# Two chained transformer models in one kernel: root tables loaded a stage ahead, norm sums before a low half, and three smaller moves

## The reference, cut to what matters

```
first_block:  h = x + short_conv_mixer(rms_norm(x));   h += conv_ffn(rms_norm(h))          # layer 0
              shared = shared_latent_kv(h)                                                # k, v, rotated key part
              h += mla_attention(rms_norm(h), shared);  h += conv_ffn(rms_norm(h))         # layer 1
              x = rms_norm(h) * final
second_block: mod = silu(c) @ w_ada + b_ada            # 6 vectors: shift, scale, gate, twice
              h = rmsnorm(x) * (1 + scale1) + shift1;  proj = h @ w_in
              y = [gated mix a | stick-breaking b | dilated windows c] @ w_out
              x += (1 + gate1) * y;  then a conv feed-forward with shift2, scale2, gate2
              out = rmsnorm(x) * g_final
rms_norm(x, g) = x * rsqrt(mean(x*x) + 1e-6) * g
```

## Time and profile before

| | |
|---|---|
| median of three runs | 1773.13 us |
| profiled execution | 1772.59 us |
| its span, first to last instruction | 1770.8 us |
| instructions | 21953 |
| TensorE busy | 97% |
| VectorE, ScalarE, GpSimd busy | 64%, 39%, 22% |
| mean granted clock of TensorE | 0.988 |
| HBM traffic | 105 GB/s |
| weight tiles | 291 x 512 KB, 3.3 us from issue to landing |

### The profile page before, as it was taken

The page is one execution under the profiler, slowest core; times in us unless marked ns, Lnnn a source line. Parts: engine busy times, 40 slices in busy tenths (PEclk is TensorE's granted clock), DMA queues, the critical chain, the costliest instruction groups (busy, mean ns, idle before and its releaser), DMA issues.

```text
span 1770.8 us, 21953 instructions
## 1 busy us (share of the span) xinstructions
PE 1719.7 (97%) x7798; PEld 1392.7 (79%) x7798; DVE 1131.6 (64%) x1438; ACT 682.6 (39%) x919; POOL 395.4 (22%) x170
## 2 busy tenths in 40 slices
PE   7999999999999999999999999999989899999997
PEld 6888788888887776878888888788647788888886
DVE  5566777776666786577777666564755677777222
ACT  4123444443324335344444322432553444444221
POOL 3444100000444430310000144444202200000443
PEclk9999999999999999999999999899999899999999
DMA  5233233223664220132332366322101232233331
GB/s 185 95 107 99 94 100 98 95 95 130 217 211 143 85 83 1 60 107 95 98 101 98 122 241 213 115 91 88 60 1 48 68 98 95 95 96 101 99 108 71
DMA packets 52042, 186.25 MB, mean 105 GB/s; under 512 B 5776, under 2 KB 5904, under 8 KB 51984
## 3 DMA queue, kind: packets, MB, share of 16 engines
q1 hardware_dynamic: 50832, 182.47, 31.0%
q10 hardware_dynamic: 1152, 2.99, 0.5%
HBM read 183.35 MB, written 2.10 MB: 105 GB/s over the span
## 4 chain that ended last, share of the span: by engine, by line
PE 89%; DVE 7%; ACT 2%; issue 1%; DMA 1%; DVEq 0%; ACTq 0%; POOL 0%; SPq 0%
PE ps L1505 27%; PE ps L1506 27%; PE ps L1507 27%; PE ps L1718 1%; PE ps L1744 1%; PE ps L1640 1%; PE ps L1642 1%; PE ps L1641 1%; DVE RAB L1080 1%; PE ps L1725 1%; DMA X<-x_in 1%; DVE acc L892 1%; PE ps L1733 0%; DVE QXL L903 0%; DVE cstat L1426 0%
## 5 line engine op out<-in xcount | busy, mean ns | idle before, releaser
L495 POOL TENSOR_TENSOR WL<-raw,WH 128x1024 fp32r<-128x1024 f32 x157 | 384.3, 2448 | 1327.7 <-ACT WH L544 1327.7
L1505 PE MATMUL ps<-XH,WH 128*128 128x512 f32 x1496 | 587.5, 393 | 15.6 <-DVE XL L903 10.2
L1506 PE MATMUL ps<-XL,WH 128*128 128x512 f32 x1496 | 583.6, 390 | 0.0
L1507 PE MATMUL ps<-XH,WL 128*128 128x512 f32 x1496 | 583.5, 390 | 0.0
L544 ACT ACTIVATE WH<-raw 128x1024 fp32r<-128x1024 f32 x291 | 308.7, 1061 | 586.5 <-PE ps L1507 551.2
L1505 PEld LDWEIGHTS ps<-XH,WH 128*128 128x128 f32 x1496 | 281.9, 188 | 79.4 <-POOL WL L495 9.8
L1507 PEld LDWEIGHTS ps<-XH,WL 128*128 128x128 f32 x1496 | 281.8, 188 | 58.9
L1506 PEld LDWEIGHTS ps<-XL,WH 128*128 128x128 f32 x1496 | 282.0, 188 | 58.6 <-issue 1.0
L1507 PE MATMUL ps<-HH,WL 128*128 128x512 f32 x528 | 205.4, 389 | 0.0
L1506 PE MATMUL ps<-HL,WH 128*128 128x512 f32 x528 | 205.4, 389 | 0.0
L1505 PE MATMUL ps<-HH,WH 128*128 128x512 f32 x528 | 205.4, 389 | 0.0
(11 more groups left out here) (262 smaller groups left out, 1905.7 us busy)
## 6 DMA issues: line engine op xcount, KB each, us to landing
raw<-w_tiles SPq DMA_DIRECT2D x291, 512.0 KB, 3.3
ada<-ada_tiles SPq DMA_DIRECT2D x32, 512.0 KB, 5.4
trig<-ada_tiles SPq DMA_DIRECT2D x16, 512.0 KB, 7.1
out_x<-X SPq DMA_DIRECT2D x8, 256.0 KB, 2.0
X<-x_in ACTq DMA_DIRECT2D x2, 512.0 KB, 8.2
X<-x_in SPq DMA_DIRECT2D x2, 512.0 KB, 8.5
RAB<-c_in SPq DMA_DIRECT2D x2, 512.0 KB, 4.6
MK<-mask_in ACTq DMA_DIRECT2D x1, 576.0 KB, 4.6
```

The costliest lines, as they stand in the source:

```text
L495: nc.gpsimd.tensor_tensor(WL[k % SPL][:, :], raw[:, k, :], f32(WH[k % SPL][:, :]), ALU.subtract).then_inc(s_lo, 1)
L1505: mm(bank, h, xh, start=first, stop=False)
L1506: mm(bank, h, xl, start=False, stop=False)
L1507: return mm(bank, lo, xh, start=False, stop=last)
```

## The change

Nothing is computed differently; instructions are moved.

1. Root's table is loaded explicitly before `residual` of DN0, WO, DN1, OUT2 and DN2, where before it came with the root itself.
2. At the end of DN1 and OUT2 the low half of the next stage's second tile comes after the reciprocal of the norm. The modulation vectors come before the last eviction of DN1 (`last=vectors`). Three DMA issues on ScalarE come after the root.
3. The masks are made after the first reciprocal of the kernel. TensorE starts attention once the first two `QN` are evicted and waits for the others from the third block on.
4. The eviction t = 3, j = 0 of UKV comes ahead of the last two `XL`.
5. In IN2 the second angle moves from k = 5 to k = 7. On ScalarE `Sin` moves from k = 6 to 8 and `Gelu` from 7 to 5.

```diff
@@ ScalarE
             up(0, "UP0", False)
+            nc.scalar.preload_act_table(ACT.Sqrt)
             residual("DN0", 3, "kv_in", N_KV)
...
             up(1, "UP1", False)
+            nc.scalar.preload_act_table(ACT.Sqrt)
             residual("DN1", 3, None, N_FIN, second=True)
+
+            act.wait_ge(s_ms, 1)
+            nc.scalar.activation(nt[:, 2:4, :], nt[:, 0:2, :], ACT.Sqrt, scale=1.0 / D).then_inc(s_root, 1)
 
             act.dma_start(MK[:, :], mask_in.bitcast(BF16)).then_inc(s_in["mask"], 16)
             act.dma_start(WS[:, :, :], wsp_in).then_inc(s_in["wsp"], 16)
             act.dma_start(posi[:, :], pos_in).then_inc(s_in["pos"], 16)
-
-            act.wait_ge(s_ms, 1)
-            nc.scalar.activation(nt[:, 2:4, :], nt[:, 0:2, :], ACT.Sqrt, scale=1.0 / D).then_inc(s_root, 1)
...
-                if k == 6:
+                if k == 8:
...                 (the two Sin)
-                if k == 7:
+                if k == 5:
...                 (the two Gelu)
@@ VectorE
+                        if last is not None and m == KD - 1:
+                            last()
                         product(M, i, per)
...
                             early_sums(n)
-                            if then is not None:
-                                low(then, 0)
                             continue
...
             inverse(N_A, rb)
+            dve.wait_ge(s_in["const"], 16)
+            v.tensor_copy(mask16[:, 0, :], cc("ident")).then_inc(s_m16, 1)
+            v.tensor_copy(mask16[:, 1, :], cc("causal_neg")).then_inc(s_m16, 1)
+            v.tensor_copy(mask16[:, 2, :], cc("strict_neg")).then_inc(s_m16, 1)
...
             for t in range(HEADS // 2):
                 for j in range(4):
+                    if (t, j) != (3, 0):
+                        latent_out(t, j)
...
                     for m in range(KQ):
+                        if m == KQ - 2:
+                            latent_out(3, 0)
                         lo_half(XH[:, m, :], XL[:, m, :], QL[:, m, :], vcol("q_norm", m), (s_lh, KKV + m + 1), s_ll)
...
-            residual("DN1", 3, None, None, N_FIN, modulation=1, second=True, then=T0["IN2"] + 1)
+            residual("DN1", 3, None, None, N_FIN, modulation=1, second=True, last=vectors)
...
             v.reciprocal(nt[:, 4:6, :], nt[:, 2:4, :]).then_inc(s_dg, 1)
+            low(T0["IN2"] + 1, 0)
             dve.wait_ge(s_bc, 2)
...
-                if k == 5:
+                if k == 7:
                     angle(RB, 0.25)
                     ch.link(v.memset(acc[:, :], 0.0))
...
-            residual("OUT2", 1, None, None, N_F2, gate=2, then=T0["UP2"] + 1)
+            residual("OUT2", 1, None, None, N_F2, gate=2)
 
             whole_sums(N_F2)
             token_inverse(N_F2)
+            low(T0["UP2"] + 1, 0)
@@ TensorE
-            pe.wait_ge(s_ev, M0["WO"])
+            pe.wait_ge(s_ev, M0["UQ"] + HEADS // 2 + 2)
             pe.wait_ge(s_m16, 3)
             for a in range(BLOCKS_A + 4):
+                if a == 2:
+                    pe.wait_ge(s_ev, M0["WO"])
```

More of the change, by code:

```diff
@@ L929, in whole_sums, with residual @@
                 v.tensor_tensor(nt[:, 0, :], nt[:, 6, :], ps[4][:, 0:4], ALU.add).then_inc(s_ms, 1)
-            def residual(phase, tiles_per_m, e, gname, n, gate=None, modulation=None, second=False, then=None):
+            def residual(phase, tiles_per_m, e, gname, n, gate=None, modulation=None, second=False, last=None):
                 per = 4 * tiles_per_m
@@ L1151, in key_rope, with latent_out @@
                     ropes[0] += 1
+            def latent_out(t, j):
+                M = M0["UKV"] + 4 * t + j
+                product(M)
+                if t < 2:
+                    v.tensor_copy(KN[:, 4 * t + j, :], ps[M % 4][:, :]).then_inc(s_ev, 1)
+                else:
+                    g = V_GROUP * (t - 2)
+                    v.tensor_copy(VT[:, g:g + V_GROUP, j * P:(j + 1) * P],
+                                  ps[M % 4][:, :].rearrange("p (h d) -> p h d", h=V_GROUP)).then_inc(s_ev, 1)
             for t in range(HEADS // 2):
                 for j in range(4):
[L1155 to L1162, removed]
+                    if (t, j) != (3, 0):
+                        latent_out(t, j)
                 if t == 0:
@@ L1181, in _ @@
                     key_rope(h - 1)
[L1184 to L1187, removed]
             def half_lo(n):
@@ L1238, in _, with vectors @@
             dve.wait_ge(s_cact, 2)
-            residual("DN1", 3, None, None, N_FIN, modulation=1, second=True, then=T0["IN2"] + 1)
[L1241 to L1247, removed]
-                ch.link(v.tensor_scalar(gm[:, row, :], mod[:, part * KD:(part + 1) * KD], 1.0, None, ALU.add))
-            ch.link(v.tensor_tensor(gm[:, 0, :], gm[:, 0, :], vec[:, V["final"][0]:V["final"][0] + KD], ALU.mult))
+            def vectors():
+                dve.wait_ge(s_ada, 6 * KD)
+                b0 = V["b_ada"][0]
+                ch.link(v.tensor_tensor(mod[:, :], mod[:, :], vec[:, b0:b0 + 6 * KD], ALU.add))
+                for row, (part, g) in enumerate(((1, "g_mix"), (4, "g_ffn"))):
+                    ch.step(v.scalar_tensor_tensor(gm[:, row, :], mod[:, part * KD:(part + 1) * KD], 1.0,
+                                                   vec[:, V[g][0]:V[g][0] + KD], ALU.add, ALU.mult))
+                for row, part in ((2, 2), (3, 5)):
+                    ch.link(v.tensor_scalar(gm[:, row, :], mod[:, part * KD:(part + 1) * KD], 1.0, None, ALU.add))
+                ch.link(v.tensor_tensor(gm[:, 0, :], gm[:, 0, :], vec[:, V["final"][0]:V["final"][0] + KD], ALU.mult))
+            residual("DN1", 3, None, None, N_FIN, modulation=1, second=True, last=vectors)
             dve.wait_ge(s_ssum, N_FIN + 2)
```

## The result

The changed kernel took 1763.53 us (median of 5 runs, 1761.55 to 1764.41) against 1773.09 for the kernel before beside it: ratio 0.9948, 95% interval 0.9938 to 0.9959. The forecast was 1767.0 in 1764.3 to 1770.3: the direction was right and the gain larger than forecast, 9.6 us by the medians where 5.7 to 6.1 were said. The profiled execution took 1763.78 us (span 1762.0), so the two spans differ by 8.8. Three executions in the batches further down, at 1939.5, 2171.9 and 3511.9 us, stood far outside the rest and are in no ratio.

The account below looks back on a forecast made before the run. TensorE, busy 1719.7 of 1770.8 us, was taken to bound the kernel. The terms summed to -5.7 us, taking 1772.6 to 1766.9, forecast as 1767.0, range 1764.3 to 1770.3 us.

Parts of the forecast that it names:

- Masks: Three casts before the first eviction cost 0.4 us (0.3 to 0.7); attention's start gains 0.7 (0.5 to 1.4).
- DKV and DQ: Root's table loads one stage before, so the root, reciprocal and `QXL` start sooner: 0.9 us gained (0.6 to 1.1).
- UKV to UQ: TensorE's first UQ matmul waits for a `VT` copy, now ahead of the last two `XL`: 0.9 us gained (0.6 to 1.0).
- Loads ahead of DN0, DN1, DN2: Each table load delays the third tile's `WL` by up to 1.28 us against 1.64 slack: cost 0 (0 to 0.9).
- first sign of being wrong: TensorE waiting for `WL` at the third tile of a DN stage would show the forecast wrong.
- DN1 to the second model: With the low half after the reciprocal and the vectors earlier, the spread starts sooner: 1.7 us gained (1.4 to 1.8).
- Input product: Second angle after the four `CB` copies: 1.32 us to win, new 0.4 wait for `AT`; 0.9 gained (0.4 to 1.4).
- OUT2 to UP2: VectorE's low-half `WL` no longer precedes the sums, so the spread begins at 1390.6: 1.0 us gained (0.8 to 1.2).
- The end: At the kernel's end the table load already hides behind the sums, so the gain is 0.
- Clock luck in my favour: Rival: earlier clock fall and return at the two quiet places save more, giving 1764.1 us; chance 0.09.
- low clock falls later: Rival: dots run wholly at half speed (+3.1, +2.3 us) and two window stretches double (3.4): 1775.7 us; chance 0.05.
- third sign of being wrong: Low-clock stretches longer than 10.3 us would show the forecast wrong.

Follow-up runs that it names:

- the repeat: The changed kernel run again, unchanged: 1762.40 us, ratio 0.9948 (0.9934 to 0.9962) against the kernel before.
- part 2: Filler matmuls added at the token norms, in the window stage, or both: before 1769.08, 1769.43, 1767.80 us; after 1762.04, 1762.76, 1760.45 us.
- the two kernels with window fillers: Before and after, each with 104 short matmuls ahead of TensorE's waits in the window stage: 1769.43 us (0.9986) and 1762.76 us (0.9952).
- part 1: Repeated transposes ahead of the window stage: before plus 1.5, 2.4, 3.4 us took 1769.61, 1771.44, 1775.30; after plus 1.95, 3.4 took 1766.73, 1767.85.
- parts 1 and 4: The delays by repeated transposes, and runs compared at equal mean clock: before and after are 5.0 us apart at 0.990, 5.1 at 0.991.
- part 3: Edits alone in before: sums 1770.74 us, tables 1770.81, angles 1767.40; and after with the mask casts put back late: 1763.88.

## Why the prediction was wrong, step by step

- *Masks*: said +0.4 and -0.7; traces +0.2 (casts start in the wait, the lower bound's reason, though that bound was 0.3) and -0.8 with the new wait of 0.7 for `SQ`. Right.
- *DKV and DQ*: said -0.9, measured -0.93 (-0.95 in the repeat); a weight load still waits 0.27 us for the late `QXL`, which delays TensorE's matmuls by 0.1. Right.
- *UKV to UQ*: said -0.9, measured -0.92. Right.
- *Loads ahead of DN0, DN1, DN2*: said 0 with 0.3 to spare; DN0 and DN1 together +0.3 in the profile, within the bounds (0 to 0.9). In the repeat of after a `WL` of 3.02 us made TensorE wait 0.2, which is the first sign of being wrong that the prediction named, at a small price:

```profile
441.90 3.02 POOL L495 TENSOR_TENSOR WL<-raw,WH 128x1024 fp32r<-128x1024 f32 x1 [1.81 <-ACT WH L544]
445.02 0.47 PE L1516 MATMUL ps<-HH,WH 128*128 128x512 f32 x1 [0.21 <-issue]
```

- *DN1 to the second model*: said -1.7, measured -1.64. Right, though only 0.6 is left where the clock falls before the last sums (part 2).
- *Input product*: said -0.9 with a new wait of 0.4 for `AT`; measured -0.87 (between the two kernels with window fillers, since the clock differed in the main pair, which shows -0.6) and +0.1 in the next stretch, the wait is 0.40. Right.
- *OUT2 to UP2*: said -1.0, measured -0.93 (between the two kernels with window fillers, 8.63 and 7.70). Right. *The end*: 0 for the edit.
- The sum of the measured parts is -5.5, said was -5.7.
- **What failed is the clock.** The step "Clock luck in my favour" priced only the two quiet places beside the edits, 2.9 us at 0.09, and those places did not pay in the profile after, with low stretches of 10.2 us at both as before. (In the repeat the first of them did: 3.4 us for 10.2, which gave 1.9 us from spread to turn.) That its 1764.1 lies near the 1763.5 measured is luck. The window stage, whose four low stretches the prediction had in a row, entered only as a loss ("each that doubles loses 1.7") in the case "low clock falls later". It was there to win as well: with one low stretch for four it took 4.8 us less, of which the end of the kernel took 1.4 back. Nothing in that stage was changed. The prediction's third sign of being wrong, a low stretch over 10.3 us, also came, at the end of the kernel: 11.7 us. The experiments show that work added ahead of the stage moves the time by more than its own length (part 1), that the surplus lies in the clock and not in the instructions (parts 1 and 4), and that one edit of 0.9 us comes with part of it in some executions (part 3). The fillers (part 2) point the same way, but their margins are within the noise. A range that held both signs of that case, some 4 us each way about 1767, would have held the time.
- *Still open*: what sets which repeats of the window loop get the lower clock. It repeats each 6.84 us in after (the transposes that wait for `PCT` begin at 1311.81, 1318.64 and 1325.49), and delays of 1.5, 2.4 and 3.4 us gave 2, 3 and 4 low units; no rule that I tried put the other kernels in order. How much of the surplus comes back in every execution of after, and how much is luck of the execution, stays open too: its ten ran at mean clocks of 0.990 to 0.992, and before reached 0.990 or 0.991 in 12 of 93.

## What to carry to other kernels

Where a stage is bound by a chain through TensorE and runs partly at the lower clock, its length is something of a lottery, which an edit ahead of it can draw again: price it both ways, as the number of its low stretches times what one costs (here some 1.5 us), before giving a range. Judge small edits by the stretch of the timeline that they touch and compare totals only at the same granted clock. Two hidden costs can stand behind each other, like the low half and the table load at OUT2: each edit alone gives 0.1 us there or nothing, and the pair gives 1.0. And look at the single executions before trusting a median of ten: it can fall between two groups.

## What was not expected of the hardware

Adding 1.5 us of matmuls made a kernel 2.5 us faster by the medians (1.9 by the ratio, 0.4 at the least). Six transposes of 128x128 took 0.85 us at the high and 1.5 at the low level, and a window stage of the same instructions took 34.7 to 39.5 us. The executions of one unchanged kernel spread over 6 us (1768.2 to 1774.6), in step with a mean clock of 0.991 to 0.987. Where the fall of the clock came 1.5 us sooner, eight matmuls for the last sums took 1.84 us in place of 1.03.
